# Order of VectorE's work in the dilated-attention slots of a two-layer encoder kernel

## The reference, cut to what matters

```
z = rms_norm(x) @ w_in               # 1024 -> 3*3*1024 (q, k, v of three groups) + memory q + gates
for each of 3 groups (window, dilation) = (128,1), (512,4), (2048,16):
    s = q k^T / sqrt(128) + bias(alibi, window)      # 8 heads of 128
    m = max(s);  p = exp(s - m);  l = sum(p);  o = (p / l) v;  lse = m + log l
y = sum over groups of softmax(lse) * o              # joins the three groups
y = y * silu(gate)
x = x + y @ w_out                                    # with a memory attention beside it
```

## Time and profile before

| | |
|---|---|
| median of three executions | 2139.26 us |
| the profiled execution | 2149.78 us |
| its span (first to last instruction) | 2148.0 us |
| mean granted TensorE clock | 0.987 |
| TensorE matmul busy | 2070.1 us, 96% |
| VectorE busy | 1137.6 us, 53% |
| ScalarE busy | 800.6 us, 37% |
| GpSimd busy | 393.7 us, 18% |

### The profile page before, as it was taken

The page is one execution under the profiler, slowest core; times in us unless marked ns, Lnnn a source line. Parts: engine busy times, 40 slices in busy tenths (PEclk is TensorE's granted clock), DMA queues, the critical chain, the costliest instruction groups (busy, mean ns, idle before and its releaser), DMA issues. The chain is left out here.

```text
span 2148.0 us, 28360 instructions
## 1 busy us (share of the span) xinstructions
PE 2070.1 (96%) x10045; PEld 1672.3 (78%) x10045; DVE 1137.6 (53%) x2011; ACT 800.6 (37%) x1456; POOL 393.7 (18%) x329
## 2 busy tenths in 40 slices
PE   7899999999999999999999899899999999999998
PEld 5678788787888788787887677687888788867786
DVE  7655464636455464636444422586878784334222
ACT  5443343434343343434334411445354543224210
POOL 2323232322223232322210011300101010000020
PEclk9999999999999999999999999899999999999998
DMA  7222212121122112221314421311111111512422
GB/s 241 65 64 61 58 50 73 51 67 49 59 64 63 55 49 73 54 64 49 123 46 156 157 59 49 104 30 30 50 31 48 35 43 40 152 58 91 137 60 97
DMA packets 208838, 155.91 MB, mean 73 GB/s; under 512 B 8379, under 2 KB 196101, under 8 KB 208134
## 3 DMA queue, kind: packets, MB, share of 16 engines
q1 hardware_dynamic: 204386, 149.25, 22.7%
q0 software_dynamic: 3584, 4.48, 1.0%
q10 hardware_dynamic: 804, 1.33, 0.2%
HBM read 130.56 MB, written 24.48 MB: 72 GB/s over the span
## 5 line engine op out<-in xcount | busy, mean ns | idle before, releaser
L286 DVE TENSOR_TENSOR w_lo<-w_raw,w_hi 128x512 fp32r<-128x512 f32 x303 | 278.2, 919 | 349.3 <-ACT w_hi L282 348.6
L210 PE MATMUL z_ps<-b_parts,w_hi 128*128 128x512 f32 x704 | 285.5, 406 | 5.4 <-ACT g_gate L220 1.8
L212 PE MATMUL z_ps<-b_parts,w_lo 128*128 128x512 f32 x704 | 279.5, 397 | 0.0
L211 PE MATMUL z_ps<-b_parts,w_hi 128*128 128x512 f32 x704 | 279.4, 397 | 0.0
L282 ACT ACTIVATE w_hi<-w_raw 128x512 fp32r<-128x512 f32 x308 | 192.7, 626 | 225.7 <-PE z_ps L315 105.4
L313 PE MATMUL z_ps<-ah_hi,w_hi 128*128 128x512 f32 x608 | 246.2, 405 | 5.9 <-ACT qkv L815 4.5
L315 PE MATMUL z_ps<-ah_hi,w_lo 128*128 128x512 f32 x608 | 241.2, 397 | 0.0
L314 PE MATMUL z_ps<-ah_lo,w_hi 128*128 128x512 f32 x608 | 240.8, 396 | 0.0
L210 PEld LDWEIGHTS z_ps<-b_parts,w_hi 128*128 128x128 f32 x704 | 133.6, 190 | 40.2 <-issue 7.7
L212 PEld LDWEIGHTS z_ps<-b_parts,w_lo 128*128 128x128 f32 x704 | 133.5, 190 | 31.7
L211 PEld LDWEIGHTS z_ps<-b_parts,w_hi 128*128 128x128 f32 x704 | 133.8, 190 | 29.9 <-issue 0.5
(11 more groups left out here) (410 smaller groups left out, 3826.5 us busy)
## 6 DMA issues: line engine op xcount, KB each, us to landing
w_raw<-in_a_win SPq DMA_DIRECT2D x220, 256.0 KB, 3.0
w_raw<-in_b_win SPq DMA_DIRECT2D x33, 512.0 KB, 4.0
y_scratch<-y SPq DMA_DIRECT2D x16, 512.0 KB, 2.7
w_raw<-in_a_wout SPq DMA_DIRECT2D x8, 768.0 KB, 5.5
w_raw<-in_b_wout SPq DMA_DIRECT2D x8, 768.0 KB, 5.7
xt_scratch<-xb SPq DMA_DIRECT2D x1, 4096.0 KB, 12.1
y_scratch<-g_gate SPq DMA_DIRECT2D x8, 512.0 KB, 3.8
b_wkv<-in_b_wmem SPq DMA_DIRECT2D x8, 512.0 KB, 6.3
```

The lines of the kernel that those rows point to most:

```text
L210: pe.matmul(z_ps[s][:, 0:width], w_hi[slot][:, k, :], hi[k][:, tok], start=(k == 0), stop=False)
L211: pe.matmul(z_ps[s][:, 0:width], w_hi[slot][:, k, :], lo[k][:, tok], start=False, stop=False)
L212: mm = pe.matmul(z_ps[s][:, 0:width], w_lo[slot][:, k, :], hi[k][:, tok], start=False, stop=(k == nk - 1))
L286: eng.tensor_tensor(op_ring(w_lo, u), op_raw[i], op_ring(w_hi, u).bitcast(F32), ALU.subtract).then_inc(lo_op, 1)
```

## The change

In each slot, VectorE's `softmax_in` and `move_values` are taken out of `attention` into a function of their own, `attention_first`, and this is called ahead of `op_split_lo(u+4)`. The evictions stay in front of everything; `join`, `scale_natural` and `finish` stay behind the low part. No instruction is added or removed, and no other engine's program changes. The softmax step of the present head and the value copies of the head before keep their own order otherwise.

```
+                    def attention_first(h, u):
+
                         if SC < u <= SC + 8:
                             softmax_in(h, u - SC - 1)
                         if u - 1 in VT:
                             move_values(h, VT[u - 1])
+
+                    def attention(h, u):
                         if u in (27, 31):
                             join(h, 1 if u == 27 else 0)
...
                             if u > 0 and (u - 1) % OPS in (3, 4, 5):
                                 evict_dve(...)
+                            if not gating:
+                                attention_first(h, u)
+                            if before is not None:
+                                attention_first(before, SLOTS_HEAD + u)
                             if u + 4 < slots or not gating:
                                 op_split_lo(dve, PAIRS_HEAD * h + (u + 4) // OPS, (u + 4) % OPS, u + 4)
                             if before is not None:
                                 attention(before, SLOTS_HEAD + u)
```

More of the change, by code:

```diff
@@ L1197, in finish, with attention_first @@
                         dve.tensor_tensor(y[:, tok], o_ps[:], gate[:, tok], ALU.mult).then_inc(y_done, 1)
-                    def attention(h, u):
+                    def attention_first(h, u):
                         if SC < u <= SC + 8:
```

## The result

The changed kernel took 2123.26 us (median of 6, 2119.69 to 2124.36), the kernel before beside it 2138.51 us (6, 2137.62 to 2141.16). The ratio is 0.9926, 95% interval [0.9913, 0.9938]: 0.74% faster, 15.3 us. The forecast was 2120.2 us, a gain of 19.1 us.

A forecast was written before the change was run, and what follows sets the result against it. TensorE was taken to bound the kernel, stopping for VectorE's results. Scores' stops -14.9, values' -4.6, allowance +0.4 make -19.1 us: 2139.3 to 2120.2 us, range 2116 to 2130 eight times in ten.

The forecast's parts named there:

- What bounds, and which stops go: In the eight heads, TensorE sets the time; its stops wait on VectorE's softmax maximum and value copy, 19.5 us.
- The softmax step's time line: Per slot, maximum done 1.9 us after the previous product's end P, bank asked for at P + 3.67: slack 1.8 us.
- The softmax step beside GpSimd: In its new place the softmax step is not slowed by GpSimd's sum: taken as 0, bound 1.9 us.
- Loss = idle of the weight load - 0.28: Rule for each TensorE stop in the heads: 34.1 us of waits in 52 stops make 19.5 us lost.
- I carry the difference, not the ratio: Whole kernel: the profiled execution's 19.1 us gain is subtracted from the plain median, 2139.3 us, giving 2120.2 us.
- Rival C: Plain runs have fewer stops than the profiled one, slot 25's low part and sum nearly tying: 2129.5 us; chance 0.10.
- rival A: All stops at scores and values go: 2120 us, own range 2117 to 2124; chance 0.66.
- Value copies: Copies ahead of the low part, mainly slot 28: gain 4.6 us less up to 0.4; slot 27's softmax 0.3 us earlier.
- Rival B: The value stops stay, slot 28's margin being small; only the scores' 14.9 us go: 2124.4 us; chance 0.12.
- Low part and the added wait: Later low part, with 8.4 us of cover, costs 0; so does slot 36's, some 3.5 us later behind a waiting copy.
- Rival E: Slower: GpSimd's sums move into slot 27 beside join, stopping slot 28 by 3.2 us per head: 2145.6 us; chance 0.05.
- Rival D: Low part, load or sum behind it, or late eviction ends last instead; time stays 2139 us within 0.2%; chance 0.07.

The follow-up runs named there:

- e7: Changed kernel with the low part behind everything in the slot, join, scaling and finish too: 2123.31 us, ratio to the kernel before 0.9910.
- e9: Changed kernel with one idle VectorE copy of 0.60 us ahead of the softmax step in slots 21 to 26: 2122.40 us.
- e10: Changed kernel with four idle VectorE copies, 2.4 us, ahead of the softmax step in slots 21 to 26: 2165.14 us, ratio 1.0109.
- e1: The kernel before, unchanged, profiled again: 2138.83 us (12 runs); the profiled execution took 2135.26 us.
- e8: The changed kernel again, no edit, on another chip: 2125.25 us, ratio 0.9925 to the kernel before at 2141.97 us.
- e2: Kernel before with only the softmax step moved ahead of the low part, value copies left behind it: 2127.99 us, ratio 0.9949.
- e11: Changed kernel with one idle VectorE copy of 0.60 us ahead of the softmax step of slot 28 alone: 2127.28 us.
- e6: Changed kernel with the one value copy of slot 36 put back behind the low part: 2125.86 us, ratio to the kernel before 0.9924.
- e4: Kernel before with only slot 25's softmax step moved ahead of the low part: 2132.82 us, ratio 0.9967.
- e5: Kernel before with GpSimd's weight sum (L269) issued before the statistics DMA (L910), VectorE's order unchanged: 2132.72 us, ratio 0.9959.

## Why the prediction was right, and where its sizes were not

**What bounds, and which stops go: right.** Both waits of the earlier trace rows went, at the places named, and no other wait took their place in the heads (rows after, e7).

**The softmax step's time line: right.** `max_done` was put at P + 1.9 us: in the changed kernel's slot 25, P is 491.87 and the second pass ends at 493.77. The bank was put at P + 3.67; it is asked for at 495.54. e9 and e10 bracket the slack.

**The softmax step beside GpSimd: right.** The changed kernel has 17 first and 16 second passes wholly under a sum, each 0.41 or 0.42 us. The Trainium skill, page "SBUF — State Buffer", section "Who interferes with whom", says that a VectorE instruction with at most one SBUF input, outside the modes that use both port pairs, does not contend with GpSimd. The trace agrees.

**Loss = idle of the weight load - 0.28: mis-sized.** It gave 19.5 us for the stops of the profiled execution; laid over each other the traces have 24.3. The term lacked what follows the stop. In the earlier trace rows it can be seen: the undisturbed L972 pair lasts 0.59 us, the one after the stop 0.70. In the first the pair's second weight load is hidden, in the second it isn't, and the next matmul starts 0.54 instead of 0.43 us later. Stop by stop, the overlay exceeds the formula by 0.11 us at each of the 31 scores' stops, and by 0.06 to 0.07 at each of the 21 values' stops: 4.8 us, the whole difference.

**From the profiled execution to the plain ones: the step that failed.** "I carry the difference, not the ratio" took the profiled execution's stops as those of the plain runs. They were not: seven of its eight heads were bad, against two of eight in e1. Rival C named this, slot and mechanism, and got 0.10. The 10.5 us between the profiled execution and the median stood in front of me unexplained, beside a mechanism that could make 1.4 us per head. The argument against C, that seven heads of eight had gone the slow way, was none: it was one execution, and the slow one. By the measured sizes, 1.36 us in every head and 2.05 more in a bad one, the 15.3 us gained are 8 x 1.36 + 2.05 x 2.1: some two bad heads in a plain run of that chip, an estimate, since those runs have no trace, and a rough one, since the traces also vary by up to 3 us ahead of the heads. On the chip of e8 the kernel before was slower and the gain 16.7 us. The two errors, 24.3 - 19.1 = 5.2 us too little for the profiled execution and 24.3 - 15.3 = 9.0 too much for the plain ones, partly cancelled. That 19.1 lies near 15.3, and the time inside rival A's own range of 2117 to 2124, is in part luck: C's mechanism was at work, though its time, 2129.5, was not met.

**Value copies: they went, by a step with one wrong sign.** Rival B is out, 1.3 of the values' 10.5 us of waits are left. But "the softmax step of slot 27 some 0.3 us earlier" has the wrong sign: join became 0.45 us later (e2), because the low part now waits behind a step whose scores aren't done. The 0.6 us from slot 28's own low part covers it, and e11 found that slot without slack. The 4.6 us ascribed to the copies were nearly all slot 28 of the bad heads: by the overlay slot 28 cost 5.2 us in the eight heads, of which 4.1 are what the seven bad heads lost beyond the 0.13 of the good one.

**Low part and the added wait cost nothing: right.** e7 puts it last, e6 takes the wait back, and over all heads they differ from the changed kernel by 0.1 and 0.6 us. Rival E is out: L1172 in slot 27 of the fourth head takes 1.18 us as before. Rival D is out too, with a remainder: no product waits for a low part, but the stop for an eviction in slot 33 of e6 (and by its place that of e8) is of its kind, 0.3 to 0.6 us in one head of eight.

**What the prediction did not ask: why slots 22 to 24 stopped.** It named GpSimd's sum for slot 25 alone. The same meeting, with the sum of L265 and the low part of slot 22, makes about 1 us of the 1.36 us that a good head loses. The gain of moving the softmax step is the same either way; but the counterexample of the fifth head was one for slot 25 only.

## What to carry to other kernels

When an engine with slack serves the engine that sets the time twice in one slot, once for now and once for four slots on, the order of the two matters even where their length does not: put first what that engine asks for next, and price the other by its distance. Before trusting one profile, ask why it differs from the median of the plain runs; if an unequal outcome from nearly equal starts is in the trace, the difference may be just the number of times it fell badly, and only the part that is there in every run can be forecast as gain. And measure a stop by laying two traces over each other, or from start to start over several instructions, not by the idle before the first.

## What the runs showed of the hardware that was not expected

A VectorE instruction with two SBUF inputs can be held by a GpSimd sum that, by the records, started after it. This happened only where the sum stood directly behind a DMA issue of GpSimd. In slot 25 of the fourth head before, beside the earlier trace rows:
```profile
506.91 0.81 POOL L910 DMA_DIRECT2D stat_mem<-nat  x1 [10.87 <-ACT work L1055]
```
First the rule, from all fourteen traces, for a low part (L286) and a sum (or GpSimd's like instruction of L928) that overlap. Where the sum started first, by 0.02 us or more, and had at least 0.2 us left, the low part ended 0.54 to 0.56 us after the sum, in all 822 cases. Where the low part started first, by up to 0.69 us, and no DMA issue stood directly ahead of the sum, it kept its 0.69 us in all 168 cases, and the sum took up to 1.84 us instead of 1.30. So the second was the one that waited, and the recorded start told which it was.

Then the exception. In e4 the low part of slot 25 started 0.09 to 0.39 us ahead of a sum directly behind the DMA issue, and was held in all eight heads, to 1.96 to 2.26 us:
```profile
500.18 2.11 DVE L286 TENSOR_TENSOR w_lo<-w_raw,w_hi 128x512 fp32r<-128x512 f32 x1
```
```profile
499.60 0.81 POOL L910 DMA_DIRECT2D stat_mem<-nat  x1 [9.18 <-ACT work L1055]
500.43 1.30 POOL L269 TENSOR_TENSOR w_raw<-w_raw 128x512 f32<-128x512 f32 x1
```
In the two traces of the kernel before, with a start 0.70 us ahead of such a sum it was long in both cases, and with 0.72 or 0.73 us long in seven and short in seven. The long ones end about 0.55 us after the sum does, as under the rule (507.75 + 1.31 = 509.06 against 507.02 + 2.60 = 509.62 in the earlier trace rows). The DMA issue alone held nothing: in e5 all eight low parts beside it kept their 0.69 us. So it is the sum behind a DMA issue, and the recorded start of one of the two is not the time from which it had its port; which of them is off, the traces do not show. Why the tie at 0.72 us falls one way or the other was not found.

The Trainium skill, page "SBUF — State Buffer", section "Who interferes with whom", says that issue order decides who blocks, and that the one that comes second is fully blocked. The traces agree, by the recorded starts, in the 990 cases of the rule; behind a DMA issue the recorded starts do not foretell who was first.
